# Numbering the places without a token out of range in the expert gathers of a decoder layer

## The reference

```python
grp = jnp.argmax(g_logits, axis=-1)                       # one of 4 groups
top_val, top_idx = lax.top_k(e_in, EXPERT_TOPK)           # 2 of its 8 experts
expert = grp[:, None] * EXPERTS_PER_GROUP + top_idx       # 32 experts
...
def block(args):
    toks, wts, e = args
    xb = h_pad[toks]
    a = xb @ w_exp_gate[e]
    u = xb @ w_exp_up[e]
    return ((jax.nn.silu(a) * u) @ w_exp_down[e]) * wts[:, None].astype(xb.dtype)
```

## Time and profile before

| | |
|---|---|
| median of 3 executions | 1528.72 us |
| the three | 1528.72, 1521.4, 1539.46 us |
| the profiled execution, its own time | 1531.23 us |
| its span from first to last instruction | 1529.5 us |
| mean granted TensorE clock | 0.945 |

### The profile page before, as it was taken

How to read it: one execution, slowest core, us unless ns; L and a number is a source line. 1 busy time by engine, 2 the same in 40 slices (tenths; PEclk the granted TensorE clock), 3 DMA queues, 4 the chain that set the end, 5 groups by cost and what they waited for, 6 DMA issues and landing times.

```text
span 1529.5 us, 20160 instructions
## 1 busy us (share of the span) xinstructions
PE 1343.2 (88%) x7755; PEld 813.0 (53%) x7755; DVE 343.4 (22%) x826; ACT 285.7 (19%) x595; POOL 217.9 (14%) x293
## 2 busy tenths in 40 slices
PE   8899999899999999999999997798788778776870
PEld 4344687454667677678888776343333323322330
DVE  2533112555332423300000125111000000100015
ACT  2100367333223323210000003000000100000001
POOL 3112333321010201110000011100000000000006
PEclk9899999978999999999999998799899999999995
DMA  9956799967625323141301627699999999999975
GB/s 329 380 213 205 245 366 331 317 251 245 198 56 170 103 76 107 49 132 49 110 1 66 196 86 247 213 378 399 394 401 405 401 390 406 401 397 392 427 292 179
DMA packets 127633, 382.44 MB, mean 250 GB/s; under 512 B 9605, under 2 KB 54934, under 8 KB 111167
## 3 DMA queue, kind: packets, MB, share of 16 engines
q1 hardware_dynamic: 105552, 308.44, 54.0%
q0 software_dynamic: 20112, 67.21, 13.8%
q10 hardware_dynamic: 1886, 5.69, 1.2%
HBM read 355.67 MB, written 27.86 MB: 251 GB/s over the span
## 4 chain that ended last, share of the span: by engine, by line
PE 69%; DMA 24%; DVE 3%; issue 1%; ACT 1%; POOL 1%; SPq 0%; POOLq 0%; ACTq 0%; DVEq 0%
PE ps L1420 62%; DMA ring<-in_w_exp_up 21%; PE ps L1431 7%; DMA h_rows<-work 1%; DVE work L1181 1%; DVE work L1414 0%; DMA hx<-expert_rows,dest_i 0%; DMA work<-in_c_sample 0%; SPq L428 0%; DVE hx L956 0%; DVE work L1413 0%; DMA work<-h_rows,idx 0%; DVE work L952 0%; POOL work L637 0%; POOL work L633 0%
## 5 line engine op out<-in xcount | busy, mean ns | idle before, releaser
L1420 PE MATMUL ps<-ring,work 128*64 128x512 f32 (+2 forms) x2720 | 422.3, 499 | 93.1 <-DMA ring<-in_w_exp_up 72.9
L1420 PEld LDWEIGHTS ps<-ring,work 128*64 128x64 f32 (+1 forms) x2720 | 151.2, 130 | 327.4 <-issue 234.5
L1420 PE MATMUL ps<-ring,hx 128*128 128x256 f32 (+3 forms) x880 | 220.8, 444 | 1.6 <-ACT hx L669 1.6
L1420 PE MATMUL ps<-hx,ring 128*128 128x272 f32 x768 | 179.1, 393 | 0.6 <-DVE work L1181 0.6
L1420 PEld LDWEIGHTS ps<-ring,hx 128*128 128x128 f32 (+1 forms) x880 | 136.1, 174 | 77.7 <-issue 64.5
L1420 PEld LDWEIGHTS ps<-hx,ring 128*128 128x128 f32 x768 | 145.2, 190 | 31.2 <-DVE work L1181 1.1
L1420 PE MATMUL ps<-work,ring 128*128 128x272 f32 x640 | 149.3, 393 | 0.0
L1420 PE MATMUL ps<-work 32*128 32x256 f32 (+11 forms) x798 | 120.2, 390 | 22.2 <-DVE work L1360 8.7
L1420 PEld LDWEIGHTS ps<-work,ring 128*128 128x128 f32 x640 | 121.2, 190 | 26.0 <-issue 1.2
L1420 PEld LDWEIGHTS ps<-work 128*32 128x32 f32 (+5 forms) x798 | 61.0, 158 | 65.4 <-issue 39.1
L875 ACT ACTIVATE work<-ps 128x256 f32<-128x256 f32 x32 | 12.3, 383 | 445.3 <-PE ps L1420 445.3
(11 more groups left out here) (281 smaller groups left out, 846.9 us busy)
## 6 DMA issues: line engine op xcount, KB each, us to landing
ring<-in_w_exp_down SPq DMA_DIRECT2D x32, 2048.0 KB, 24.4
ring<-in_w_exp_gate SPq DMA_DIRECT2D x31, 2048.0 KB, 18.7
ring<-in_w_exp_up SPq DMA_DIRECT2D x31, 2048.0 KB, 25.1
ring<-in_w_ada SPq DMA_DIRECT2D x12, 2048.0 KB, 19.6
ring<-in_cache_k SPq DMA_DIRECT2D x64, 256.0 KB, 4.7
ring<-in_cache_k POOLq DMA_DIRECT2D x64, 256.0 KB, 5.0
ring<-in_cache_v SPq DMA_DIRECT2D x64, 256.0 KB, 4.8
ring<-in_cache_v POOLq DMA_DIRECT2D x64, 256.0 KB, 5.0
```

Source lines behind the costliest of these rows:

```text
L1420: return pe.matmul(out, lhsT, rhs, start=start, stop=stop, **k)
```

## The change

Three things are altered. The constant that the place array is multiplied with is now the token's number plus 1 (`token_number`, same shape). The conversion to int32 subtracts 1 in the same instruction, so that a place with a token still gets its number, and a place without one gets -1. And both gathers from `h2_dram`, that of the 32 blocks and that of the further blocks, are given 543 as the highest valid index, and told that an index out of range is no error: such a row is to be left out, and the 4 KB of its partition in `xs` stay as they are. All that an engine does before and after, its order and its waits are the same; on VectorE one conversion has become one `TENSOR_SCALAR` of the same shape.

```diff
-    c["token_id"] = np.where(tok < NT, tok, 0)
+    c["token_number"] = np.where(tok < NT, tok + 1, 0)
...
                 pool.indirect_dma_start(xs[e % 4], None, h2_dram[:, :],
-                                        bass.IndirectOffsetOnAxis(ap=idx[:, e:e + 1], axis=0)).then_inc(s(f"xs_in{e % 4}"), 16)
+                                        bass.IndirectOffsetOnAxis(ap=idx[:, e:e + 1], axis=0),
+                                        bounds_check=NT - 1, oob_is_err=False).then_inc(s(f"xs_in{e % 4}"), 16)
...
                 pool.indirect_dma_start(xs[0], None, h2_dram[:, :],
-                                        bass.IndirectOffsetOnAxis(ap=idx_cur[:, 0:1], axis=0)).then_inc(s("xs_in0"), 16)
+                                        bass.IndirectOffsetOnAxis(ap=idx_cur[:, 0:1], axis=0),
+                                        bounds_check=NT - 1, oob_is_err=False).then_inc(s("xs_in0"), 16)
...
             for c in range(2):
-                last = dve.tensor_tensor(rh[:, c], rh[:, c], bc(const("token_id").unsqueeze(2), [P, 5, CAP]), ALU.mult)
+                last = dve.tensor_tensor(rh[:, c], rh[:, c], bc(const("token_number").unsqueeze(2), [P, 5, CAP]), ALU.mult)
             last.then_inc(*done("idx_hot"))
             dve.wait_ge(*after("idx_ps"))
-            dve.tensor_copy(idx[:, :], ps[0:CAP, 6, 0:EB]).then_inc(*done("idx_ready"))
+            dve.tensor_scalar(idx[:, :], ps[0:CAP, 6, 0:EB], -1.0, None, ALU.add).then_inc(*done("idx_ready"))
```

## The result

The changed kernel takes 1515.33 us (median of 6 executions, 1507.92 to 1520.14), the kernel before 1530.78 us (6 executions). The ratio is 0.9889, 95% interval 0.9845 to 0.9933: 17.0 us less, 10 to 24 with the interval. The forecast was 18 us less.

What follows compares the result with a forecast made beforehand. The expert stage was taken as bound by full DMA engines. 18 us saved on 27 gathers, with 0 for head, GpSimd and VectorE, took 1531.23 to 1513 us, median 1511; the 8-in-10 range was 1494 to 1531.

Steps and rivals of the forecast that it cites:

- The bound: Expert stage, 980 to 1476 us: DMA engines are full, so it ends when its bytes have been moved.
- The change skips: Expert gathers: places without a token, index -1, are not fetched; gathers' bytes fall 46%, 7.08 to about 3.8 MB.
- The rival of a signed comparison: Gathers' limit: -1 passes as a signed number below it, so nothing is skipped; 1529 us, 11% with packets sent anyway.
- Cost of a gather, 1.67 us: Expert stage: 27 gathers cost the full DMA engines 45 us, 1.67 us each, though their bytes need only 16.7 us.
- The share that goes, 14.2 to 20.7 us, taken as 18: Expert stage: 20.7 us saved if cost falls with rows, 14.2 if uneven relief loses part; 18 us taken.
- The discount for uneven relief: Expert stage: loads wait for all 16 engines, so half of 13.0 us relief of slowing may be lost, leaving 14.2 us.
- Head: First gather, on the chain: may land 0.5 us earlier, index test may cost as much; 0, with -0.5 to +1 us.
- GpSimd and VectorE, cost 0: Gather issue on GpSimd and index conversion on VectorE: the limit and the subtraction of 1 add 0 us.
- The fullest share: Gathers dealt to engines in blocks of four rows; engines 0 to 4 keep their load: gain 0 to 5 us, 1526, 22%.
- The first row: Gathers: 960 requests to one 4 KB row are what is dear; 25 to 36 us go, 1499 us, 12%.
- Stretches beside gathers towards 370 GB/s, rounds 32.9 us, 424 GB/s without gathers: Expert-stage signs: rate beside gathers rises from about 310 GB/s, chain rounds fall from 34.3 us, gather-free rate stays.
- Why gathers are dear: Gathers into 64 partitions: something shared slows them, as 64 partitions reach 8 of 16 ports; 187 GB/s alone.

Runs made afterwards that it cites:

- e6: Changed kernel, but each gather fetches 32 fixed rows at places with n // 2 even, so eight engines have 4 rows each, eight none: 0.9919 of the kernel before.
- e1: Changed kernel, but every gather fetches the same 64 different rows, none skipped or fetched twice: 1.0038 of the kernel before.
- e2: Changed kernel, but all 64 places of every gather fetch the table's first row: 1.0013 of the kernel before.
- e9: Changed kernel, but each gather fetches 128 different fixed rows of 2 KB into 128 partitions, none skipped: 0.9837 of the kernel before.

## Why the prediction was right

- *The bound.* The stage ends when its bytes are moved: yes. Without gathers 47 us go, the rounds fall to 30.8 us, and the DMA engines stay full (0.99 in the last 10 us too). In the changed kernel they stay full up to the last 10 us, and there they don't (0.87).
- *The change skips.* The gathers' bytes fell by the forecast 46% (3.83 MB; 3.8 was forecast). The rival of a signed comparison is out. The skipped places are still sent, as packets of 4 bytes. The prediction named that only as a way in which nothing would be gained; it costs next to nothing.
- *Cost of a gather, 1.67 us.* Measured 1.69 by taking all of them away. (The 434 GB/s beside it stands in no line of the earlier trace rows, whose highest is 432; nothing hangs on it.)
- *The share that goes, 14.2 to 20.7 us, taken as 18.* Measured 17 by the times, and in the profiled executions 20.1 from the first gather to the last load, 0.9 of it at the head. The proportional value (0.46 x 1.69 = 0.78 us) is what the queue's row shows (0.82). The discount for uneven relief had a right reason and too large a size: uneven places do cost (12 in place of 21 us at the extreme of e6), but in the changed kernel all that is seen of it is the 1.2 us at the end, of which even dealing brings back 1.0. So the mechanism was right, and that 18 came within 1 us of 17.0 is partly luck: the interval of 10 to 24 us holds the proportional 20.7 as well, and the queue's row and the profiled execution are nearer to that. The middle of 14.2 and 20.7 is also 17.5 and not 18.
- *Head.* 0 was counted, with -0.5 to +1 us. The first gather now lands after 2.93 us, not 3.80, a gain of 0.9 us, more than the 0.5 us that it was given for half of its rows.
- *GpSimd and VectorE, cost 0.* Right: 43 ns more a gather, hidden but for the first, and 199 ns for the subtraction in place of 200, hidden.
- *The fullest share (22%).* Not the result here, but not nothing: it appears when rows sit on half of the engines. The drift of landings in the changed kernel, to 9.9 us apart where they were 3.6, is its trace. The prediction's picture of it, blocks of four rows to an engine, is not what the trace fits: it fits pairs.
- *The first row (12%).* Refuted by e1 and e2.
- *Stretches beside gathers towards 370 GB/s, rounds 32.9 us, 424 GB/s without gathers.* 376 and 354; 32.8; 423 while loads are queued, but 411 from 1423 us to the last landing, which is the one sign that failed.
- *Why gathers are dear.* "Something shared slows them when 64 partitions are filled" came out true, but the 187 GB/s from which it was inferred don't show it: gathers alone into 128 partitions moved 170. That 187 lies near the 196 GB/s set beside it says nothing either. e9 against e1 shows that it is the partitions.

## What to carry to other kernels

Where the DMA engines are full over a whole stage, a transfer's price is what the stage's main queue loses by it, and that can be near three times its bytes' share; read it as bytes of the main queue over the rate of a stretch without the transfer. Places without data in an indirect DMA can be numbered out of range and so left out, which takes off their share of that price. Look first at whether such a transfer reaches both halves of the partitions: short rows over all 128 gained more (25 us, 0.66 us left of a gather) than skipping did over 64 (17 us, 0.87 left), and the two gains overlap. And look at the end of the stage, where engines with uneven shares no longer finish together.

## What the runs showed of the hardware

- A row left out by its index is still a packet of 4 bytes: 2160 packets in both kernels, 3.83 against 7.08 MB.
- 256 KB gathered into 128 partitions beside a full weight queue cost 0.66 us, into partitions 0 to 63 1.65 us, with as many packets of the same size (80 a gather). 128 KB cost 0.83 us in partitions 0 to 31 and 0.74 in 0 to 63.
- Two gathered rows of 2 KB go as one packet of 4 KB: 20112 packets with 128 such rows a gather, as with 64 rows of 4 KB, and 19088 with 64.
- Engines with less to do run ahead of the others for as long as loads are queued: the 16 landings of one load moved from 3.3 us apart at 1032 us to 9.9 us apart at 1450 us in the changed kernel, and stayed at 3.6 us for most loads, 5.7 at most, in the kernel before from 1063 us on. At the end of the stage that left the engines idle for some 1.2 of the last 10 us more than before.
